# Memory rows and weights in four pieces between the token tiles, and the input norm's weight and bias applied at the eviction of the turned rows

## What is computed

```python
xp = layer_norm(x_prompt, ln_in_g, ln_in_b)      # 512 x 1024
xs = layer_norm(x_sample, ln_in_g, ln_in_b)      # 8 x 1024
# mem_kv = mem_prompt @ w_mem_kv                 # 256 x 1024 by 1024 x 512
z = x @ p['w_in']                                # 1024 x 2816 columns, then gates
```

## Time and profile before

| | us |
|---|---|
| median of 3 runs | 1399.42 (1396.41 to 1400.54) |
| the profiled execution, launch time | 1398.44 |
| its span | 1396.6 |
| TensorE busy | 1146.1 (82% of the span) |
| VectorE, ScalarE, GpSimd busy | 436.1, 238.7, 109.9 |
| from the start to the first product of the projection loop | 43.70 |
| the projection loop (22 column tiles) | 43.70 to 198.42 |

### The profile page before, as it was taken

How to read it: one execution, slowest core, us unless ns; L and a number is a source line. 1 busy time by engine, 2 the same in 40 slices (tenths; PEclk the granted TensorE clock), 3 DMA queues, 4 the chain that set the end, 5 groups by cost and what they waited for, 6 DMA issues and landing times.

```text
span 1396.6 us, 21853 instructions
## 1 busy us (share of the span) xinstructions
PE 1146.1 (82%) x9283; PEld 796.6 (57%) x9283; DVE 436.1 (31%) x797; ACT 238.7 (17%) x400; POOL 109.9 (8%) x97
## 2 busy tenths in 40 slices
PE   4999989998989999998999836878787887878740
PEld 2788876777568878866864333434344443444320
DVE  5000003675446667433323271111111111111137
ACT  3100011244311121021111101111111111111001
POOL 3000000000000000000001101111111111111103
PEclk9999999999799999999999957999999999999975
DMA  7342242222130112153554034999999999999951
GB/s 276 121 150 75 75 138 72 71 68 68 31 77 25 48 30 54 46 198 114 201 198 176 31 152 136 390 426 425 426 416 424 414 425 418 414 420 420 420 201 61
DMA packets 47164, 290.78 MB, mean 208 GB/s; under 512 B 9204, under 2 KB 11318, under 8 KB 34027
## 3 DMA queue, kind: packets, MB, share of 16 engines
q1 hardware_dynamic: 41922, 281.41, 51.9%
q0 software_dynamic: 5184, 8.54, 1.8%
HBM read 274.97 MB, written 24.23 MB: 214 GB/s over the span
## 4 chain that ended last, share of the span: by engine, by line
PE 62%; DMA 25%; DVE 5%; issue 2%; ACT 2%; DVEq 1%; SPq 1%; POOL 0%; POOLq 0%; ACTq 0%
PE psum L646 59%; DMA arena<-in_e_up 17%; DMA arena<-in_e_gate 5%; PE psum L651 3%; DVE arena L1423 3%; DVE arena L1426 2%; ACT arena L1182 1%; DMA arena<-in_w_mem_kv 1%; DMA arena<-scratch_x,arena 1%; DMA arena<-in_p_abm 0%; SPq L627 0%; DVEq L2021 0%; POOL arena L2034 0%; SPq L623 0%; DVE arena L1441 0%
## 5 line engine op out<-in xcount | busy, mean ns | idle before, releaser
L646 PE MATMUL psum<-arena 64*64 64x64 f32 (+8 forms) x8760 | 1077.3, 341 | 155.5 <-DMA arena<-in_e_gate 60.6
L646 PEld LDWEIGHTS psum<-arena 64*64 64x64 f32 (+4 forms) x8760 | 738.1, 153 | 471.8 <-issue 214.2
L1182 ACT ACTIVATE arena<-psum 128x512 f32<-128x512 f32 (+8 forms) x151 | 94.6, 648 | 684.4 <-PE psum L646 397.1
L1423 DVE TENSOR_TENSOR arena<-arena,psum 128x256 f32<-128x256 f32 (+3 forms) x136 | 74.5, 548 | 403.5 <-PE psum L646 210.1
L1423 DVE TENSOR_TENSOR arena<-arena 128x1024 f32<-128x1024 f32 (+17 forms) x168 | 125.7, 758 | 195.8 <-PE psum L646 164.1
L651 PE MATMUL psum<-arena 128*128 128x128 f32 (+4 forms) x523 | 79.3, 288 | 42.6 <-DMA arena<-in_mem_prompt 13.3
L651 PEld LDWEIGHTS psum<-arena 128*128 128x128 f32 (+4 forms) x523 | 59.0, 151 | 74.8 <-issue 49.0
L2034 POOL TENSOR_TENSOR arena<-arena 128x1024 f32<-128x1024 f32 (+1 forms) x15 | 37.1, 2474 | 517.0 <-DVE arena L1423 517.0
L1423 DVE TENSOR_TENSOR arena<-psum,arena 128x256 f32<-128x256 f32 (+4 forms) x85 | 47.0, 564 | 66.8 <-PE psum L646 66.4
L2077 POOL DMA_INDIRECT arena<-scratch_x,arena x32 | 32.7, 1023 | 300.9 <-DVE arena L1972 300.3
L1401 ACT ACTIVATE arena<-psum 128x256 f32<-128x256 f32 x32 | 12.3, 383 | 247.7 <-PE psum L646 247.7
(11 more groups left out here) (105 smaller groups left out, 155.7 us busy)
## 6 DMA issues: line engine op xcount, KB each, us to landing
arena<-in_e_gate SPq DMA_DIRECT2D x32, 2048.0 KB, 16.8
arena<-in_e_up SPq DMA_DIRECT2D x32, 2048.0 KB, 21.9
arena<-in_e_down SPq DMA_DIRECT2D x32, 2048.0 KB, 12.6
arena<-in_w_in SPq DMA_DIRECT2D x46, 512.0 KB, 4.0
scratch_gates<-arena SPq DMA_DIRECT2D x24, 260.0 KB, 4.1
arena<-scratch_gates SPq DMA_DIRECT2D x8, 780.0 KB, 4.9
arena<-in_p_abm SPq DMA_DIRECT2D x8, 640.0 KB, 5.9
scratch_x<-arena SPq DMA_DIRECT2D x8, 512.0 KB
```

What stands on the lines that cost most here:

```text
L646: return pe.matmul(out, a, b, start=start, stop=stop)
L1182: return act.activation(out, a, ACT.Copy)
L1423: return v.tensor_tensor(out, a, b, op)
```

## The change

- The memory rows come in already turned (`mem_T`, 128 x 8 x 256), so their transposes, evictions and `memtok` go. `mem_T` and `w_mem_kv` are loaded in four pieces (`mem_piece(k)`, two of the eight chunks each), interleaved with the token tiles. PE multiplies each piece as it arrives, accumulating both halves side by side in banks 4 and 5, with token turns 0, 1 and 2 behind pieces 1, 2 and 3.
- The token tiles are turned when they are scaled (`x_scaled`), without weight and bias. These are applied where the turned rows leave PSUM: a feature is then a partition, so they are one scalar for each partition (`lnT`, 128 x 16). ACT evicts four column blocks of each tile with four activations, DVE the other four with four tensor_scalar instructions (`xT_half`).
- The rows themselves still get weight and bias (they are needed later), but by DVE behind its evictions, and POOL after it; the `gb` loads move behind the first two `w_in` loads.
- The turns of the memory keys, and ACT's copy to `mkT`, move behind the projection loop.

```diff
@@ -432,15 +433,32 @@
                 sp.dma_start(xtok[0:rows(t), t, :], src).then_inc(s[f"tile{t}_in"], 16)
 
             first = C0 + P + 2
+            w_mem = I["w_mem_kv"].rearrange("(p c) n -> p c n", c=KD)
+
+            def p1_tile(f, q, need):
+                sp.wait_ge(s["z_made"], need)
+                sp.dma_start(p1w[q], I["w_in"][bass.ds(f, 1)].rearrange("a p c n -> (a p) c n")).then_inc(s[f"p1w{q}_in"], 16)
+
+            def mem_piece(k):
+                c = slice(2 * k, 2 * k + 2)
+                sp.dma_start(memT[:, c, :], I["mem_T"][:, c, :]).then_inc(s[f"mkv{k}_in"], 16)
+                sp.dma_start(wmem[:, c, :], w_mem[:, c, :]).then_inc(s[f"mkv{k}_in"], 16)
+
+            mem_piece(0)
             x_load(0)
             sp.dma_start(view(C0, P + 2), I["consts"][:, 0:P + 2]).then_inc(s["ident_in"], 16)
-            sp.dma_start(gb[:, 0, :], I["ln_in_g"].partition_broadcast(P)).then_inc(s["x_in"], 16)
-            sp.dma_start(gb[:, 1, :], I["ln_in_b"].partition_broadcast(P)).then_inc(s["x_in"], 16)
+            sp.dma_start(lnT, I["ln_in_T"]).then_inc(s["ident_in"], 16)
+            mem_piece(1)
             x_load(1)
-            sp.dma_start(memtok, I["mem_prompt"].rearrange("(t p) d -> p t d", p=P)).then_inc(s["mem_in"], 16)
-            for t in range(2, Q):
-                x_load(t)
-            sp.dma_start(wmem, I["w_mem_kv"].rearrange("(p c) n -> p c n", c=KD)).then_inc(s["wmem_in"], 16)
+            x_load(2)
+            mem_piece(2)
+            x_load(3)
+            x_load(4)
+            mem_piece(3)
+            p1_tile(0, 0, 1)
+            p1_tile(1, 1, 2)
+            sp.dma_start(gb[:, 0, :], I["ln_in_g"].partition_broadcast(P)).then_inc(s["consts_in"], 16)
+            sp.dma_start(gb[:, 1, :], I["ln_in_b"].partition_broadcast(P)).then_inc(s["consts_in"], 16)
             sp.dma_start(view(first, NCONST - P - 2), I["consts"][:, P + 2:]).then_inc(s["consts_in"], 16)
             sp.dma_start(prow[0:PR_N, :], I["params"]).then_inc(s["params_in"], 16)
             sp.dma_start(ssraw[0:B, :], I["state_shift"]).then_inc(s["params_in"], 16)
...
             for f in range(2 * PIECES + 2):
-                p1_tile(f, f % 2, f + 1)
+                if f >= 2:
+                    p1_tile(f, f % 2, f + 1)
                 if f == 1:
                     sp.wait_ge(s["mkv_made"], 2)
                 if f % 2 and f // 2 < PIECES:
@@ -659,38 +674,33 @@
                 last.then_inc(s["gate_made"], 1)
 
             pe.sem_inc(s["z_made"], 2)
-            pe.wait_ge(s["ident_in"], 16)
 
             def turn_x(t):
                 n = rows(t)
-                pe.wait_ge(s["x_normed"], t + 1)
+                if t == 0:
+                    pe.wait_ge(s["ident_in"], 32)
+                pe.wait_ge(s["x_scaled"], t + 1)
                 if t >= 2:
                     pe.wait_ge(s["xT_ready"], t - 1)
+                    pe.wait_ge(s["xT_half"], t - 1)
                 for c in range(KD):
                     last = turn(bank(2 * (t % 2), KD, P)[:, c, 0:n], xtok[0:n, t, c::KD])
                 last.then_inc(s["x_turned"], 1)
 
 
-            pe.wait_ge(s["mem_in"], 16)
-            for t in range(2):
-                for c in range(KD):
-                    last = turn(bank(4 + 2 * t, KD, P)[:, c, :], memtok[:, t, c::KD])
-                last.then_inc(s["mem_turned"], 1)
-            pe.wait_ge(s["memT_ready"], 2)
-            pe.wait_ge(s["wmem_in"], 16)
-            for t in range(2):
-                for c in range(KD):
-                    last = mm(bank(4 + t, 512), memT[:, c, t * P:(t + 1) * P], wmem[:, c, :], c == 0, c == KD - 1)
-                last.then_inc(s["mkv_made"], 1)
-                for u in ((0, 1), (2, 3, 4))[t]:
-                    turn_x(u)
-            pe.wait_ge(s["mkv_ready"], 2)
-            for f in range(2):
-                for t in range(2):
-                    last = turn(bank(6, 2, NMEM)[:, f, t * P:(t + 1) * P], mkv[:, t, f * P:(f + 1) * P])
-            last.then_inc(s["mkv_made"], 1)
-
+            for k in range(KD // 2):
+                pe.wait_ge(s[f"mkv{k}_in"], 32)
+                for c in range(2 * k, 2 * k + 2):
+                    for t in range(2):
+                        last = mm(bank(4 + t, 512), memT[:, c, t * P:(t + 1) * P], wmem[:, c, :], c == 0, c == KD - 1)
+                        if c == KD - 1:
+                            last.then_inc(s["mkv_made"], 1)
+                if k:
+                    turn_x(k - 1)
+            for u in range(KD // 2 - 1, Q):
+                turn_x(u)
             pe.wait_ge(s["xT_ready"], Q)
+            pe.wait_ge(s["xT_half"], Q)
             with pe.Fori(0, NF // 2) as i:
                 for q in range(2):
                     pe.wait_ge(s[f"p1w{q}_in"], i * 16 + 16)
@@ -699,6 +709,12 @@
                         for c in range(KD):
                             last = mm(bank(2 * q + h, NH), p1w[q][:, c, :], xT[:, c, h * NH:(h + 1) * NH], c == 0, c == KD - 1)
                     last.then_inc(s["z_made"], 1)
+            pe.wait_ge(s["mkv_ready"], 2)
+            for f in range(2):
+                for t in range(2):
+                    last = turn(bank(6, 2, NMEM)[:, f, t * P:(t + 1) * P], mkv[:, t, f * P:(f + 1) * P])
+            last.then_inc(s["mkv_made"], 1)
+
             pe.wait_ge(s["z_ready"], NF + 2)
             pe.wait_ge(s["mkT_ready"], 1)
...
+            act.wait_ge(s["ident_in"], 32)
 
             def x_turned(t):
                 n = rows(t)
+                if t == 0:
+                    act.wait_ge(s["ident_in"], 32)
                 act.wait_ge(s["x_turned"], t + 1)
-                copy(xT[:, :, t * P:t * P + n], bank(2 * (t % 2), KD, P)[:, :, 0:n]).then_inc(s["xT_ready"], 1)
-
-            def mem_turned(t):
-                if t < 2:
-                    act.wait_ge(s["mem_turned"], t + 1)
-                    copy(memT[:, :, t * P:(t + 1) * P], bank(4 + 2 * t, KD, P)).then_inc(s["memT_ready"], 1)
-
-            layer_norm(xtok, 0, 1, after=lambda t: mem_turned(t - 1) if t >= 1 else None)
+                for c in range(KD // 2, KD):
+                    last = act.activation(xT[:, c, t * P:t * P + n], bank(2 * (t % 2), KD, P)[:, c, 0:n], ACT.Identity,
+                                          bias=lnT[:, 1, c:c + 1], scale=lnT[:, 0, c:c + 1])
+                last.then_inc(s["xT_ready"], 1)
+
+            layer_norm(xtok, 0, 0, after=lambda t: x_turned(t - 2) if t >= 2 else None)
+            x_turned(Q - 2)
+            x_turned(Q - 1)
             for t in range(2):
                 act.wait_ge(s["mkv_made"], t + 1)
                 copy(mkv[:, t, :], bank(4 + t, 512)).then_inc(s["mkv_ready"], 1)
-                for u in ((0, 1), (2, 3, 4))[t]:
-                    x_turned(u)
-            act.wait_ge(s["mkv_made"], 3)
-            copy(mkT, bank(6, 2, NMEM)).then_inc(s["mkT_ready"], 1)
             act.sem_inc(s["z_ready"], 2)
             with act.Fori(0, NF // 2) as i:
                 for q in range(2):
                     act.wait_ge(s["z_made"], i * 2 + q + 3)
                     copy(z[:, bass.ds(i * 2 + q, 1), :].rearrange("p a (h n) -> p (a h) n", h=2),
                          psum[:, 2 * q:2 * q + 2, 0:NH]).then_inc(s["z_ready"], 1)
+            act.wait_ge(s["mkv_made"], 3)
+            copy(mkT, bank(6, 2, NMEM)).then_inc(s["mkT_ready"], 1)
...
-            def rows_in(t, at):
-                v.wait_ge(s[f"tile{t}_in"], 16)
-                if t == 2:
-                    v.wait_ge(s["x_in"], 32)
-
-            layer_norm(xtok, 0, rows_in, 1)
+            for t in range(Q + 2):
+                if t < Q:
+                    n = rows(t)
+                    v.wait_ge(s[f"tile{t}_in"], 16)
+                    for h in range(2):
+                        v.bn_stats(st6[0:n, t, h, :], xtok[0:n, t, h * 512:(h + 1) * 512])
+                    v.drain()
+                    v.bn_aggr(mv[0:n, t, :], st6[0:n, t, :, :]).then_inc(s["ln_stats"], 1)
+                    v.wait_ge(s["ln_std"], t + 1)
+                    v.reciprocal(rstd[0:n, t, :], rstd[0:n, t, :])
+                    v.drain()
+                    stt(nmr[0:n, t, :], mv[0:n, t, 0:1], -1.0, rstd[0:n, t, :], ALU.mult, ALU.mult).then_inc(s["ln_rs"], 1)
+                u = t - 2
+                if u >= 0:
+                    n = rows(u)
+                    v.wait_ge(s["x_turned"], u + 1)
+                    if u == 0:
+                        v.wait_ge(s["ident_in"], 32)
+                    for c in range(KD // 2):
+                        last = ts(xT[:, c, u * P:u * P + n], bank(2 * (u % 2), KD, P)[:, c, 0:n], lnT[:, 0, c:c + 1], ALU.mult,
+                                  lnT[:, 1, c:c + 1], ALU.add)
+                    last.then_inc(s["xT_half"], 1)
+            v.wait_ge(s["consts_in"], 48)
+            for t in range(Q):
+                n = rows(t)
+                tt(xtok[0:n, t, :], xtok[0:n, t, :], gb[0:n, 0, :], ALU.mult).then_inc(s["ln_gained"], 1)
 
 
```

(3 more changed lines are left out.)

22 lines of the change are left out of this document (10 added, 12 removed).

## The result

| | before | after |
|---|---|---|
| median of 4 runs, us | 1397.91 (1396.06 to 1400.54) | 1384.39 (1377.12 to 1387.88) |
| ratio | | 0.9895, 95% interval 0.9851 to 0.9939 |
| the profiled execution, launch time (span) | 1398.44 (1396.6) | 1377.12 (1375.3) |
| first product of the projection loop | 43.70 | 29.35 |
| end of the loop | 198.42 | 184.07 |

What follows compares the result with a forecast made beforehand. TensorE, holding 62% of the chain, was taken as the bound, idle early until `w_mem_kv` landed at 21.16 us. 1398.44 - 14.5 + 0.6 = 1384.5 for the profiled execution, median 1.0 above: forecast 1385.5, range 1381 to 1391.

Steps and rivals of the forecast that it cites:

- TensorE's start: At the head, the first product starts at 5.2 us, when piece 0 is usable, instead of 21.16.
- No wait up to turn 3: In the head, each piece lands 2 to 3 us before it is wanted; turns 2 and 3 end at 25.4 us.
- The low clock in the first products: At TensorE's start, the clock stays low for 6 us: 7 MATMULs at 0.86 us, the other 25 at 0.43.
- Evictions: Turned tiles leaving PSUM: four take ACT 1.3 us (bounds 0.8 and 1.85) and DVE 1.15.
- The tail's chain: End of the head: small tile scaled at 24.9 us, its turns end at 27.2, projection loop starts at 29.2.
- The gain at the head: Before the projection loop: its start moves from 43.70 to 29.2 us, a gain of 14.5.
- Given back behind the loop: After the projection loop: one more 128 x 512 ACT copy ahead of the memory keys' turns costs 0.6 us.
- Sum at the end of the loop: Through the projection loop's end: 14.5 us gained at the head, less 0.6 given back, 13.9 in all.
- a stage that has stretched: Sign of being wrong: a stage after the head takes longer than before; the projection loop was to last 154.7 us.
- unbroken low clock: Rival: in the new head the clock stays low throughout, losing 7.5 us, 1393; chance 7%.
- late piece: Rival: in the head, late pieces or slow evictions lose some 4 to 6 us, 1390.5; chance 8%.
- price of 1.1 us for a transfer: Rival: queued head transfers each cost time; no gain at 1.1 us each, 1405 us at 1.5; chance 2%.

Runs made afterwards that it cites:

- second and third profile: The changed kernel unedited, timed and profiled twice more; medians 1381.83 and 1383.57 us, ratios 0.9901 and 0.9913 to the kernel before.
- pieces only: Changed kernel with the old norm put back (whole-row weight and bias ahead of the turns, gb loaded early); 1391.0 us, ratio 0.9952 to the kernel before.
- keys in the head: Changed kernel with the memory keys' turns and ACT's copy of them back ahead of the projection loop; 1386.24 us, ratio 0.9929 to the kernel before.
- the last kernel: Its sibling with ACT's and DVE's evictions one tile later and two fill products instead of three at the end; 1384.45 us, ratio 0.9920 to the kernel before.
- its sibling: Changed kernel plus five zero products ahead of piece 0, five products filling waits, and z_ready raised before ACT's copies; 1379.48 us, ratio 0.9879 to the kernel before.
- more transfers: Changed kernel with each of the eight memory transfers cut in two; 1384.31 us, ratio 0.9905 to the kernel before.
- zeros ahead of piece 0: Changed kernel with five unread 128x256 products of zeros, written by DVE, ahead of piece 0; 1384.86 us, ratio 0.9914 to the kernel before.

## Why the prediction was right, step by step

- **TensorE's start**: 5.2 forecast, 5.66 measured (5.55 to 5.69 in the other profiles with piece 0 unsplit). The count of bytes along the old curve held to half a microsecond, though the new curve has other slices.
- **No wait up to turn 3**: as forecast, turn 3 ended near 25.6 (25.4).
- **The low clock in the first products**: forecast 6 us. The same 16 MATMULs took between 8.56 and 10.09 us in the profiles of the changed kernel and its variants without zeros, so the loss against 16 x 0.43 was 1.7 to 3.2 us, where 3.0 was in the sum. This comes from the length of the products alone. The forecast's sign, a low PEclk there, cannot be read: the column says 1.00 from 5.7 to 15.7 us while the first MATMULs took 0.85 us each.
- **Evictions**: four by themselves take ACT 1.49 us (forecast 1.3, bounds 0.8 and 1.85) and DVE 1.37 (1.15), so both sizes were low. In the tail it didn't matter: consecutive ones overlap, and ACT's eight of tiles 2 and 3 took 2.55 us for the 2.6 put down.
- **The tail's chain**: forecast 24.9 for the end of the small tile's scaling, 25.29 measured (24.05 + 1.24); small turns to end at 27.2, 27.77 measured; loop at 29.2, 29.35 measured. The chain ran 0.4 us late up to ACT's copies (28.91 for 28.5) and won 0.3 back there, since the loop began 0.44 us behind the first copy's start for 0.7. That is a small piece of luck in the last figure. The gain at the head is 14.35 us for 14.5.
- **Given back behind the loop**: 0.53 us for 0.6.
- **Sum at the end of the loop**, up to the side turns: 13.82 us (199.21 - 185.39) for 13.9.
- **What the sum did not have**: the loop's first products at the low clock. The new waits of 1.12 and 1.57 us, which the forecast had named as waits and priced as time only, cost about 2.5 us more in most executions. The paragraph on rivals looked for the low clock in the first products and in later stages, not here; of the signs of being wrong, a stage that has stretched did show, in the second and third profile. With this term the sum would give some 11.4 us, at least where the kernel before keeps the full clock in the loop. By the medians of the three timings the gain is 13.5 (1397.91 - 1384.39), 13.4 (1395.2 - 1381.83) and 11.4 us (1394.93 - 1383.57), all under the 13.9 without it. So that the median came out 1.1 us from the forecast is in part luck: executions differ by more than this term, and the forecast's base, the 1399.42 of three runs, became 1397.91 with a fourth.
- **The 7.5 us beyond it in the first profile.** By the starts in the chain, 13.8 us had grown to 15.1 at the group of 56 MATMULs (356.85, 341.71), to 19.7 behind it, and to 21.1 at 607.71. The rows of after, then those of before, then the group in the second and the third profile of the changed kernel (the chain's row counts 55 of the 56):

```profile
341.71 19.26 PE psum L661 x56
361.65 11.00 PE psum L661 x48
...
586.66 28.66 PE psum L661 x128
```

```profile
381.34 11.00 PE psum L646 x48
...
607.71 28.66 PE psum L646 x128
```

```profile
347.20 23.76 PE psum L661 x55
```

```profile
344.87 23.74 PE psum L661 x55
```

The group took 19.26 us for 23.80: the same MATMULs, so the low clock was some 9 us shorter, twice the 4.5 us. Of all thirteen profiles three show 19.26, and they are the three that lie 6 to 9 us under their kernels' medians (this one, "pieces only" and "keys in the head"); the other ten show 23.73 to 23.82. That the later excess was the clock of that execution and no effect of the change is what the two further profiles of the unedited kernel say: the group at 23.76 and 23.74, and spans of 1385.5 and 1381.9. Between the first and the second profile of it, 10.2 us apart, three stretches hold nearly all of the difference: the loop (2.5), the stretch from its end to this group (3.1) and the group (4.5); what lies behind is equal (1013.7 and 1014.0 us).
- **The rivals.** None came about: no unbroken low clock, no late piece, no price of 1.1 us for a transfer, the point of no gain. Whether a gain at the head can steer the clock of later stages (the last kernel's 5 us over its sibling may be that) stays open; its executions are too few to separate it from chance.

## What to carry to other kernels

When one wait holds an engine, work out what would hold it next before pricing the cure: here the weights' arrival hid the norm's chain on other engines, and each cure alone gave 0 to 4 us of the 13. Split a load when its consumer can begin on a part, and put the first part at the very front; transfers queued behind others cost about 0.1 us each here, but two more in front of the first use cost 1.3. When a change leaves TensorE short waits right ahead of a long dense stage, price them with the clock too: they may cost more in the stage than in themselves, and products into an unused bank covered them in the three profiles that had them, though no median shows the gain by itself. And when one engine's chain is shortened, look for the one that lies just behind it: 2.7 us taken from TensorE's low clock gave 0.6.

## What the runs showed of the hardware that was not expected

- Short waits with eight small turns between them (1.12 and 1.57 us in the changed kernel) were followed by a low clock in eight of nine profiles, for some 2 to 6 us of the loop (twice the excess of 155.92 to 157.69 us over 154.72). In six of them it fell ahead of the loop, in two ("more transfers", "zeros ahead of piece 0") within the loop's first 2 us, whose mean clock was 0.67 and 0.75 behind 1.00 in the last 2 us of the head.
- An unedited kernel's executions differ by up to 11.9 us (1375.97 to 1387.88 over 15 runs), more than the kernel before did (1391.26 to 1400.54 over all its runs, on several chips), and the two profiles compared above put the difference into stretches at the low clock.
- A float32 eviction of 128 x 128 with two operands for each partition took ACT 442 ns and DVE 404 ns (means of 16), not much less than the 460 and 417 ns of the 128 x 256 forms in the earlier trace rows. Consecutive ones overlap: four took 1.49 and 1.37 us.
